# First expert's tokens as the one-hot product writes them: turned, in 24 products into two banks

## The chip, the cores and the metric

One core of one Trainium2 chip. The time is the device time of one execution, in microseconds (us); the median of three runs counts. TensorE, VectorE, ScalarE, GpSimd and SyncE run their own instruction streams and wait for each other on semaphores.

## What is computed

One step of a two-layer decoder trunk, for 256 prompt tokens and 8 sample tokens (264 in all, of width 1024). Each layer is a mixer (layer 0: gated DeltaNet and mLSTM heads, layer 1: S5), a LayerNorm, a mixture of 16 experts, and a LayerNorm. The change is in the mixture of experts:

```python
def moe(x, router_w, router_b, w_gate, w_up, w_down):
    logits = jnp.einsum('bld,de->ble', x.astype(F32), router_w.astype(F32))
    probs = jax.nn.softmax(logits, axis=-1)
    ...                       # best group, top-2 experts in it, weights comb
    hid = jax.nn.silu(jnp.einsum('bld,edf->blef', x, w_gate)) * jnp.einsum('bld,edf->blef', x, w_up)
    hid = hid * comb[..., None].astype(hid.dtype)
    return jnp.einsum('blef,efd->bld', hid, w_down)
```

## The kernel before

Everything is fp32; the program issues one product, and the profile shows two matmul passes for it (one for a transpose). The 264 tokens lie in three tiles, 128, 128 and 8 rows. Each expert works on up to SLOT = 64 tokens at a time: their rows are gathered, turned into features by 128-column chunks (DC = 8 chunks), multiplied by gate and up weights (L1934 and L1935, 8 chunks each, on the two halves of the array), gated (silu on ScalarE, L1989, product on VectorE, L2018), turned again (L1881), multiplied by the down weights (L1958, L1959), evicted to `ypair`, and spread back to the tokens by a product (L1976, L1980) for each pair of experts.

For experts 1 to 15 the rows come by an indirect DMA of GpSimd (L2042) from `x_dram`, a copy of the rows in DRAM that SyncE's queue stores in three transfers (L1816, called x_rows); `xg` holds them, and PE turns them in `pe_tokens` (L1881) into bank 4, from where ScalarE copies them to `xgT` (L1985).

Expert 0 doesn't wait for the gather. While routing is worked out (`route_pe`, `route_dve`), VectorE makes `first_slot` (L1761), a one-hot matrix of tokens by slots, for the first expert. `pe_first_rows` (L1895) multiplies it with `xperm`, the permuted rows: 3 tiles by 2 halves, 6 products, with the one-hot matrix as the weights (64 columns) and 512 columns of `xperm` moved. The result, the 64 gathered rows, lies in bank 7, columns 0 to 511 on partitions 0 to 63 and the rest on partitions 64 to 127. ScalarE copies one half (L1903) and VectorE the other (L1909) to `first_rows`, which lies in `ypair[0]`. `xperm` lies over the same memory, so both copies first wait until x_rows has been read out (`x_rows` 48). Then `pe_first_tokens` turns the rows by eight transposes (L1881), and `act_tokens` copies bank 4 to `xgT[0]` (L1985). Gate/up of expert 0 waits for that.

The order on PE is written out by hand: `route_pe` issues the mask products (L1632 to L1636), fillers (`keep_busy`, L311: products of 512 columns whose result nobody reads), `pe_first_rows`, the list product (L1642, 6 products, from which VectorE makes the indices of all gathers, L1789 and L1791), and then `moe_pe` issues the first tokens, gate/up of expert 0, `route_sel_pe` (L1650), the tokens of expert 1, and so on. VectorE does `dve_first_rows` between `lists` (L1765) and the weights and indices. ScalarE does `act_first_rows` and `act_tokens` ahead of its loop over experts.

The weights of an expert (two halves of gate and up, 1 MB each of four, and 2 MB of down) are loaded by SyncE's queue into three slots in layer 1 and fewer in layer 0; a load from expert 3 on is issued when PE has released the slot (`gu_half`, `gu_done`, `down_done`).

Of the kernel before, what the change touches and what calls it, by code (L numbers as in the profile page):

```python
# [89 lines left out]
def build(nc, io, out, book):  # L90

    ctx = ExitStack()
    with ctx:
# [3 lines left out]
        def sem(name):  # L97
            if name not in sems:
                sems[name] = ctx.enter_context(nc.semaphore(name))
            return sems[name]  # L100
# [26 lines left out]
        def tok(t):  # L127

            return P if t < TT else NS
# [1487 lines left out]
        def route_pe(t, tag):  # L1617
            t.wait_ge(sem("router_in"), 32)
            for i in range(TT):
                t.wait_ge(*ac.at(f"{tag}xT_in{i}"))  # L1620
                for k in range(DC):
                    nc.tensor.matmul(ps[:, 1, i * NE:(i + 1) * NE], xT[:, k, i * P:(i + 1) * P], router[:, k], start=k == 0, stop=k == DC - 1)
            xT_rest_pe(t, tag)
            t.wait_ge(*dv.at(f"{tag}xT_rest"))
            for k in range(DC):
                last = nc.tensor.matmul(ps[0:NS, 1, TT * NE:3 * NE], xT[:, k, SEQ:], router[:, k], start=k == 0, stop=k == DC - 1)
            last.then_inc(*pe.done(f"{tag}logits"))
            keep_busy(0, 6)
            t.wait_ge(*dv.at(f"{tag}mask"))
            flat_mask = rt(9, 48)  # L1630

            nc.tensor.matmul(ps[:, 1, 0:48], before, flat_mask, start=True, stop=False)  # L1632
            t.wait_ge(*dv.at(f"{tag}tiles_so_far"))
            nc.tensor.matmul(ps[:, 1, 0:48], ones, rt(4, 48), start=False, stop=True).then_inc(*pe.done(f"{tag}pos"))
            t.wait_ge(*dv.at(f"{tag}all_tiles"))
            nc.tensor.matmul(ps[:, 6, 256:256 + NE], ones, rt(5, 48)[:, 0:NE], start=True, stop=True).then_inc(*pe.done(f"{tag}total"))  # L1636

            keep_busy(0, 2)
            pe_first_rows(t, tag)
            t.wait_ge(*dv.at(f"{tag}lists"))  # L1640
            for n in range(6):
                last = nc.tensor.matmul(ps[0:SLOT, 1, 128:128 + LISTS], at_slot[:, n], list_value[:, n], start=n == 0, stop=n == 5)  # L1642
            last.then_inc(*pe.done(f"{tag}lists"))
# [14 lines left out]
        def route_dve(v, tag):  # L1658
# [104 lines left out]
            v.wait_ge(*dv.last())  # L1763
            per_list = lambda a: a.rearrange("p i j -> p (i j)").unsqueeze(2).to_broadcast([P, 6, LISTS])
            nc.vector.tensor_tensor(list_value, in_list, per_list(value_f), ALU.mult).then_inc(*dv.done(f"{tag}lists"))  # L1765
            dve_first_rows(v, tag, 0 if tag == "n0" else 1)
            weight, both = rt(6, 3, 2), rt(0, 48)[:, 0:3]
            for j in range(2):
                nc.vector.tensor_tensor(rt(10 + j), hot[j], e, ALU.mult).then_inc(*dv.done())  # L1769
# [112 lines left out]
                          **(dict(start=True, stop=True) if c == 0 else {}))  # L1882
            last.then_inc(signal, 1)

        first_rows = ypair[0][0:SLOT]

        def pe_first_rows(t, tag):

            for i in range(3):
                t.wait_ge(*po.at(f"{tag}rows{i}"))  # L1890
            t.wait_ge(*dv.at(f"{tag}first_slot"))
            for i in range(3):
                n = tok(i)
                for half in range(2):
                    last = nc.tensor.matmul(ps[SLOT * half:SLOT * half + SLOT, 7, :], first_slot[0:n, i, 0], xperm[0:n, i, 512 * half:512 * half + 512],  # L1895
                                            start=i == 0, stop=i == 2)
            last.then_inc(*pe.done(f"{tag}first_rows"))

        def act_first_rows(a, tag, l):

            a.wait_ge(sem(f"x_rows{l}"), 48)
            a.wait_ge(*pe.at(f"{tag}first_rows"))
            nc.scalar.copy(first_rows[:, 0:512], ps[0:SLOT, 7, :]).then_inc(*ac.done(f"{tag}first_rows"))  # L1903

        def dve_first_rows(v, tag, l):

            v.wait_ge(sem(f"x_rows{l}"), 48)
            v.wait_ge(*pe.at(f"{tag}first_rows"))
            nc.vector.tensor_copy(first_rows[:, 512:D], ps[SLOT:P, 7, :]).then_inc(*dv.done(f"{tag}first_rows"))  # L1909

        def pe_first_tokens(t, tag, l):

            t.wait_ge(*ac.at(f"{tag}first_rows"))
            t.wait_ge(*dv.at(f"{tag}first_rows"))
            to_features(ps[:, 4], first_rows, DC, sem(f"tokens_done{l}"))

        def pe_tokens(t, l, k, u, s):

# [6 lines left out]
        def pe_gate_up(t, l, k, u, s):  # L1925
            w = waits(t, l)
            w("xgT_done", k + 1)
            if later(k):
                w("hid_done", k)
            slot, nth = gu_slot(l, k, u, s)  # L1930
            for c in range(DC):
                if c % 4 == 0:
                    t.wait_ge(sem(f"w_gu{c // 4}{slot}_{l}"), nth * 32)
                nc.tensor.matmul(ps[0:SLOT, 5, :], xgT[s][:, c], gate_w[slot][:, c], start=c == 0, stop=c == DC - 1)  # L1934
                last = nc.tensor.matmul(ps[SLOT:P, 5, :], xgT[s][:, c], up_w[slot][:, c], start=c == 0, stop=c == DC - 1)  # L1935
                if c == 3:
                    last.then_inc(sem(f"gu_half{l}"), 1)
            last.then_inc(sem(f"gu_done{l}"), 1)
# [44 lines left out]
        def act_tokens(a, l, k, u, s):  # L1983
            waits(a, l)("tokens_done", k + 1)
            nc.scalar.copy(xgT[s].rearrange("p a b -> p (a b)"), ps[:, 4, :]).then_inc(sem(f"xgT_done{l}"), 1)  # L1985
# [69 lines left out]
        def at_expert(k):  # L2055

            return k, k // 2, k % 2
# [38 lines left out]

        def moe_pe(t, tag, l):

            pe_first_tokens(t, tag, l)
            for k in range(NE):  # L2100
                pe_gate_up(t, l, *at_expert(k))
                if k == 0:
                    route_sel_pe(t, tag)
                if k % 2 == 1 and k >= 3:
                    pe_combine(t, l, k // 2 - 1, k - 2, slice(0, P), (k // 2 - 1) % 2)
                if k + 1 < NE:
                    pe_tokens(t, l, *at_expert(k + 1))
                if k > 0:
                    pe_down(t, l, *at_expert(k - 1))
                pe_units(t, l, *at_expert(k))  # L2110
                if k == 0:
                    t.wait_ge(*dv.at(f"{tag}sel"))
                    residual_pe(t, 0, 0)
            pe_down(t, l, *at_expert(NE - 1))

            def more(k, e, u, s):
                for part in (pe_tokens, pe_gate_up, pe_units, pe_down):
                    part(t, l, k, u, s)
                pe_combine(t, l, None, k, slice(SLOT * s, SLOT * s + SLOT), 0)
            further_rounds(t, tag, more)  # L2120
            pe_combine(t, l, PAIRS - 1, NE - 1, slice(0, P), (PAIRS - 1) % 2)

        def moe_act(a, tag, l):

            act_first_rows(a, tag, l)
            act_tokens(a, l, *at_expert(0))
            a.wait_ge(*dv.at(f"{tag}list_sel"))
            for k in range(NE):
                act_silu(a, l, *at_expert(k))
                if l == 0 and k == NE // 2:  # L2130
                    ln_load(a, "ln_ffn_g", "ln_ffn_b", 0, "n0")
                if k + 1 < NE:
                    act_tokens(a, l, *at_expert(k + 1))
                if k > 0:
                    act_y(a, l, *at_expert(k - 1))
            act_y(a, l, *at_expert(NE - 1))

            def more(k, e, u, s):
                for part in (act_tokens, act_silu, act_y):
                    part(a, l, k, u, s)  # L2140
            further_rounds(a, tag, more)

        def moe_dve(v, tag, l):

            for k in range(NE):
                dve_hid(v, l, *at_expert(k))
                if k == 0:
                    route_sel(v, tag)
                if k > 0:
                    dve_y(v, l, *at_expert(k - 1))  # L2150
                dve_hidT(v, l, *at_expert(k))
                dve_spread(v, l, k, k % 2, (sel[:, 0, k:k + 1], sel[:, 1, k:k + 1]))
                if l == 0 and k == 2:
                    s5_turn_start(v)
                if l == 0 and 3 <= k < 15:
                    s5_turn_step(v, (k - 3) // 2, (k - 3) % 2)
            dve_y(v, l, *at_expert(NE - 1))

            def more(k, e, u, s):
                for part in (dve_hid, dve_hidT, dve_y):  # L2160
                    part(v, l, k, u, s)
                dve_spread(v, l, k, s, (selc[:, 0:1], selc[:, 1:2]))
            further_rounds(v, tag, more)
            waits(v, l)("combined", NE)
            with if_crowded(v, tag):
                waits(v, l)("combined", NE * ROUNDS)
# [677 lines left out]
```

## Time and profile before

| | |
|---|---|
| median of 3 runs | 963.6 us (963.37 to 964.43) |
| profiled execution | 964.52 us |
| its span | 962.7 us |
| PE busy | 890.9 us (93%) |
| PE weight loads busy | 478.0 us (50%) |
| VectorE busy | 395.9 us (41%) |
| ScalarE busy | 172.7 us (18%) |
| GpSimd busy | 216.9 us (23%) |
| mean granted clock of TensorE | 0.956 of full speed |
| moved by DMA | 277.32 MB, mean 288 GB/s |

Busy PE is not PE at its peak, since matmuls are pipelined and thin ones wait for their weight loads. The page's rows of 40 slices cover 24 us each; a digit is the busy share in tenths. The chain of work that ended last says where time is on the path, and the granted clock by stretch says at which of its two levels (1.2 or 2.4 GHz) TensorE ran there. Layer 0's experts run from about 300 to 557 us, layer 1's from about 708 us to the end.

### The profile page before, as it was taken

The numbers are of one execution on the slowest core, as the hardware profiler recorded it, in microseconds if no ns is written. First come the engines' busy times: TensorE is split into PE (matmuls) and PEld (weight loads), VectorE is DVE, ScalarE is ACT, GpSimd is POOL, SyncE is SP. The second block draws the span as 40 slices with busy tenths as digits, with TensorE's granted clock in tenths as the row PEclk, the third lists the DMA queues.
The fourth block names the chain that finished last, engine by engine and source line by source line (L and its number), as shares of the span: only waits on it lengthen the run. The fifth ranks groups of instructions, "written<-read, shape, count | busy, mean of one in ns | idle before, by whom it ended". The sixth has DMA issues, their size and how long they took to land.

```text
span 962.7 us, 13215 instructions
## 1 busy us (share of the span) xinstructions
PE 890.9 (93%) x5404; PEld 478.0 (50%) x5404; DVE 395.9 (41%) x812; ACT 172.7 (18%) x310; POOL 216.9 (23%) x322
## 2 busy tenths in 40 slices
PE   8899998998997999899989769999799999999992
PEld 5788887984463433333333258644543333333330
DVE  4489845735645212122233267844252212121125
ACT  0402234223020111111101143012101111111011
POOL 4469997301120510101000020001102100110000
PEclk9999999997988999999999988999799999999997
DMA  9527655903969879999999947466939999999952
GB/s 272 113 93 261 224 175 151 294 13 114 316 231 380 343 291 353 405 412 404 401 405 425 413 173 209 142 237 243 364 137 355 417 400 402 399 409 406 408 243 90
DMA packets 100830, 277.32 MB, mean 288 GB/s; under 512 B 25368, under 2 KB 61670, under 8 KB 80150
## 3 DMA queue, kind: packets, MB, share of 16 engines
q1 hardware_dynamic: 89882, 256.26, 70.6%
q10 hardware_dynamic: 8484, 16.09, 4.9%
q0 software_dynamic: 2400, 4.07, 1.4%
q8 instruction: 46, 0.75, 0.3%
q14 instruction: 18, 0.15, 0.0%
HBM read 260.97 MB, written 18.01 MB: 290 GB/s over the span
## 4 chain that ended last, share of the span: by engine, by line
PE 78%; DMA 9%; DVE 8%; ACT 2%; issue 2%; SPq 0%; POOL 0%; DVEq 0%; ACTq 0%
PE ps L1934 21%; PE ps L361 11%; PE ps L1958 10%; DMA ring<-in_moe_w_up 6%; PE ps L2629 5%; PE ps L1976 5%; PE ps L1881 4%; PE ps L864 3%; DMA x_rows<-work 2%; PE ps L2493 2%; PE ps L2509 1%; PE ps L1571 1%; PE ps L1980 1%; DVE work L1534 1%; DVE work L1518 1%
## 5 line engine op out<-in xcount | busy, mean ns | idle before, releaser
L1934 PE MATMUL ps<-ring,work 128*64 128x512 f32 x416 | 187.3, 602 | 5.4 <-DMA ring<-in_moe_w_up 4.0
L1935 PE MATMUL ps<-ring,work 128*64 128x512 f32 x416 | 187.3, 603 | 0.0
L361 PE MATMUL ps<-work,ring 128*128 128x264 f32 x512 | 118.7, 392 | 3.0 <-ACT work L468 3.0
L2018 DVE TENSOR_TENSOR work<-ps,work 64x512 f32<-64x512 f32 x32 | 33.7, 1054 | 207.2 <-ACT work L1989 207.2
L1934 PEld LDWEIGHTS ps<-ring,work 128*64 128x64 f32 x416 | 55.2, 138 | 115.4 <-issue 106.1
L361 PEld LDWEIGHTS ps<-work,ring 128*128 128x128 f32 x512 | 97.3, 192 | 21.4 <-ACT work L468 3.4
L1958 PE MATMUL ps<-ring,work 128*64 128x512 f32 x216 | 100.1, 607 | 7.0 <-issue 5.6
L1959 PE MATMUL ps<-ring,work 128*64 128x512 f32 x216 | 100.2, 607 | 0.0
L1334 POOL TENSOR_TENSOR ring<-ring 128x512 f32<-128x512 f32 (+5 forms) x76 | 93.2, 1242 | 10.8 <-DVE ring L1330 7.5
L2028 DVE COPY work<-ps 64x512 f32<-64x512 f32 x32 | 22.2, 694 | 157.3 <-PE ps L1959 157.3
L2039 POOL COPY work<-work 64x1 int32<-64x1 int32 x30 | 6.1, 202 | 324.2 <-PE ps L1881 277.9
L1976 PE MATMUL ps<-work 128*128 128x512 f32 x128 | 59.3, 605 | 4.5 <-issue 3.7
L1881 PEld LDWEIGHTS ps<-const,work 64*128 64x128 f32 x448 | 39.1, 161 | 48.1 <-issue 43.0
L1989 ACT ACTIVATE work<-ps 64x512 f32<-64x512 f32 x32 | 18.8, 589 | 220.2 <-PE ps L1935 220.2
L2629 PE MATMUL ps<-ring,work 128*128 128x512 f32 x128 | 57.4, 597 | 0.6 <-DMA ring<-in_s_w_glu_b 0.6
L1958 PEld LDWEIGHTS ps<-ring,work 128*64 128x64 f32 x216 | 27.7, 138 | 56.4 <-issue 53.3
L1935 PEld LDWEIGHTS ps<-ring,work 128*64 128x64 f32 x416 | 55.2, 138 | 0.0
L1881 PE MATMUL ps<-const,work 64*128 64x64 f32 x448 | 47.8, 244 | 4.6 <-DVE work L1769 3.1
L1976 PEld LDWEIGHTS ps<-work 128*128 128x128 f32 x128 | 23.0, 189 | 40.0 <-issue 40.0
L1934 PE MATMUL ps<-work 128*64 128x512 f32 x96 | 42.6, 595 | 0.0
L1935 PE MATMUL ps<-work 128*64 128x512 f32 x96 | 42.6, 595 | 0.0
L532 DVE SCALAR_TENSOR_TENSOR work<-work 128x256 f32<-128x256 f32 x36 | 40.3, 1120 | 1.3
(488 smaller groups left out, 1213.2 us busy)
## 6 DMA issues: line engine op xcount, KB each, us to landing
ring<-in_moe_w_down SPq DMA_DIRECT2D x27, 2048.0 KB, 19.1
ring<-in_moe_w_gate SPq DMA_DIRECT2D x52, 1024.0 KB, 12.4
ring<-in_moe_w_up SPq DMA_DIRECT2D x52, 1024.0 KB, 14.6
ring<-in_w_in ACTq DMA_DIRECT2D x6, 2048.0 KB, 8.6
work<-in_moe_w_gate SPq DMA_DIRECT2D x12, 1024.0 KB, 16.9
work<-in_moe_w_up SPq DMA_DIRECT2D x12, 1024.0 KB, 19.1
work<-in_moe_w_down SPq DMA_DIRECT2D x5, 2048.0 KB, 22.5
s_out_mats<-ring SPq DMA_DIRECT2D x8, 640.0 KB, 5.1
```

What stands on the lines that cost most here:

```text
L361: last = nc.tensor.matmul(ps[:, proj_bank(j), 0:T], win[g % 2][:, k, (j % 4) * P:(j % 4 + 1) * P], xT[:, k], start=k == 0, stop=k == DC - 1)
L532: nc.vector.scalar_tensor_tensor(y, raw[:, c, w:w + SEQ], convT[:, c, 24 + w:25 + w], y, ALU.mult, ALU.add).then_inc(*dv.done())
L864: last = nc.tensor.matmul(ps[:, 2 * i + n, :], rows_of(oT[:, k], i), wout[:, k, n * 512:(n + 1) * 512], start=False, stop=k == 7)
L1334: tt = lambda o, a, b, op, name=None: nc.gpsimd.tensor_tensor(o, a, b, op).then_inc(*po.done(name))
L1881: last = op(bank[:, c * SLOT:(c + 1) * SLOT], rows[0:SLOT, c * P:(c + 1) * P], ident[0:SLOT, 0:SLOT], **(dict(start=True, stop=True) if c ...
L1934: nc.tensor.matmul(ps[0:SLOT, 5, :], xgT[s][:, c], gate_w[slot][:, c], start=c == 0, stop=c == DC - 1)
L1935: last = nc.tensor.matmul(ps[SLOT:P, 5, :], xgT[s][:, c], up_w[slot][:, c], start=c == 0, stop=c == DC - 1)
L1958: nc.tensor.matmul(ps[0:SLOT, 7, :], hidT[s][:, c], down_w[l][slot][:, c, 0:512], start=c == 0, stop=c == 3)
L1959: last = nc.tensor.matmul(ps[SLOT:P, 7, :], hidT[s][:, c], down_w[l][slot][:, c, 512:D], start=c == 0, stop=c == 3)
L1976: last = nc.tensor.matmul(ps[:, 2 * i + n, :], S[rows, i * P:(i + 1) * P], y[rows, 512 * n:512 * n + 512], **flags)
L2018: nc.vector.tensor_tensor(hid[s][0:SLOT].rearrange("t (c p) -> t p c", c=4), strided(ps[SLOT:P, 5, :]), strided(sg[s][SLOT:P]), ALU.mult). ...
L2629: last = nc.tensor.matmul(ps[:, GLU_BANK[h, i][ab], :], gyT[:, k, i * P:(i + 1) * P], glu_w(h, k)[:, ab], start=k == 0, stop=k == DC - 1)
```

## The change

`pe_first_tokens` now makes the turned tokens directly: for each chunk c of 128 features and each tile i, `xperm`'s 128 columns are the weights and the 64 columns of the one-hot matrix are moved. That is 24 products. Chunks 0 to 3 go to bank 4 and raise `tokens_done`; chunks 4 to 7 go to bank 7 and raise `first_tokens`. ScalarE copies the first bank to `xgT[0][:, 0:4]`, VectorE the second to `xgT[0][:, 4:8]`; gate/up of expert 0 waits for the second before its chunk 4. The gathered rows, their two copies, the eight transposes and the copy behind them are gone. The waits for x_rows move: on ScalarE ahead of `act_silu` of expert 1, on VectorE behind `route_sel`, ahead of the first write to `hidT`. The call stands where `pe_first_rows` stood, ahead of the list product; `moe_pe` no longer begins with the transposes.

```diff
-            pe_first_rows(t, tag)
+            pe_first_tokens(t, tag, int(tag == "n2"))
...
-            dve_first_rows(v, tag, 0 if tag == "n0" else 1)
+            dve_first_tokens(v, tag)
...
-        def pe_first_rows(t, tag):
+        def pe_first_tokens(t, tag, l):
 
             for i in range(3):
                 t.wait_ge(*po.at(f"{tag}rows{i}"))
             t.wait_ge(*dv.at(f"{tag}first_slot"))
-            for i in range(3):
-                n = tok(i)
-                for half in range(2):
-                    last = nc.tensor.matmul(ps[SLOT * half:SLOT * half + SLOT, 7, :], first_slot[0:n, i, 0], xperm[0:n, i, 512 * half:512 * half + 512],
-                                            start=i == 0, stop=i == 2)
-            last.then_inc(*pe.done(f"{tag}first_rows"))
-
-        def act_first_rows(a, tag, l):
-
-            a.wait_ge(sem(f"x_rows{l}"), 48)
-            a.wait_ge(*pe.at(f"{tag}first_rows"))
-            nc.scalar.copy(first_rows[:, 0:512], ps[0:SLOT, 7, :]).then_inc(*ac.done(f"{tag}first_rows"))
...
-        def pe_first_tokens(t, tag, l):
-
-            t.wait_ge(*ac.at(f"{tag}first_rows"))
-            t.wait_ge(*dv.at(f"{tag}first_rows"))
-            to_features(ps[:, 4], first_rows, DC, sem(f"tokens_done{l}"))
+            for c in range(DC):
+                for i in range(3):
+                    n = tok(i)
+                    last = nc.tensor.matmul(ps[:, 4 + 3 * (c // 4), (c % 4) * SLOT:(c % 4 + 1) * SLOT], xperm[0:n, i, c * P:(c + 1) * P],
+                                            first_slot[0:n, i, 0], start=i == 0, stop=i == 2)
+                if c == 3:
+                    last.then_inc(sem(f"tokens_done{l}"), 1)
+            last.then_inc(*pe.done(f"{tag}first_tokens"))
+
+        def act_first_tokens(a, l):
+
+            waits(a, l)("tokens_done", 1)
+            nc.scalar.copy(xgT[0][:, 0:4].rearrange("p a b -> p (a b)"), ps[:, 4, 0:4 * SLOT]).then_inc(sem(f"xgT_done{l}"), 1)
+
+        def dve_first_tokens(v, tag):
+
+            v.wait_ge(*pe.at(f"{tag}first_tokens"))
+            nc.vector.tensor_copy(xgT[0][:, 4:8].rearrange("p a b -> p (a b)"), ps[:, 7, 0:4 * SLOT]).then_inc(*dv.done(f"{tag}first_tokens"))
...
+                if isinstance(k, int) and k == 0 and c == 4:
+                    t.wait_ge(*dv.at(f"n{2 * l}first_tokens"))
...
-            pe_first_tokens(t, tag, l)
...
-            act_first_rows(a, tag, l)
-            act_tokens(a, l, *at_expert(0))
+            act_first_tokens(a, l)
             a.wait_ge(*dv.at(f"{tag}list_sel"))
             for k in range(NE):
+                if k == 1:
+                    a.wait_ge(sem(f"x_rows{l}"), 48)
                 act_silu(a, l, *at_expert(k))
...
                     route_sel(v, tag)
+                    v.wait_ge(sem(f"x_rows{l}"), 48)
```

## Rows read from the trace of the kernel before

**Rows 1.** The page: granted clock in 40 slices of 24 us.

```profile
PEclk9999999997988999999999988999799999999997
```

**Rows 2.** Chain that ended last, layer 0: start us, us, what.

```profile
284.13 19.75 DMA x_rows<-work
...
306.56 1.11 PE ps L1934
307.68 0.85 PE ps L1934
```

**Rows 3.** Timeline, layer 0: start us, us, engine, line, op, tiles, count [idle before].

```profile
297.73 2.94 PE L1895 MATMUL ps<-work 128*64 128x512 f32 x12 [1.43 <-DVE work L1761]
...
300.60 1.04 PE L1642 MATMUL ps<-work 128*64 128x80 f32 x12
...
303.90 0.69 DVE L1909 COPY work<-ps 64x512 f32<-64x512 f32 x1 [5.06 <-DMA x_rows<-work]
...
307.89 1.20 POOL L2042 DMA_INDIRECT work<-x_rows,work  x1 [0.23 <-issue]
...
316.10 1.81 PE L1650 MATMUL ps<-work 128*64 128x160 f32 x24
...
317.83 0.87 PE L1881 MATMUL ps<-const,work 64*128 64x64 f32 x9
```

**Rows 4.** Line 2042, the gather issued at 307.9: issue to landing.

```profile
DMA to landing us min/median/max: 6.6/6.6/6.6
```

**Rows 5.** Timeline, layer 1.

```profile
708.66 2.94 PE L1895 MATMUL ps<-work 128*64 128x512 f32 x12 [1.27 <-DVE work L1761]
...
711.53 1.04 PE L1642 MATMUL ps<-work 128*64 128x80 f32 x12
...
714.07 0.64 PE L1934 MATMUL ps<-ring,work 128*64 128x512 f32 x1 [0.68 <-ACT work L1985]
```

**Rows 6.** Single lines: duration ns min/median/max, first and last start, forms.

```profile
L735 PE MATMUL ps<-const,ring x16: 175/256/256, 205.3 to 206.9; 128*128 128x8 f32 x16
...
L383 PE MATMUL ps<-work,const x8: 277/278/278, 64.3 to 65.1; 4*128 4x40 f32 x8
...
L2023 DVE COPY work<-ps x32: 424/425/425, 320.2 to 937.4; 128x256 f32<-128x256 f32 x32
```

**Rows 7.** By stretch: us, PE, PEld, DVE, ACT, POOL busy, PEclk, DMA share, GB/s.

```profile
279.00:281.00 2.00, 2.00 (x19) 2.00 (x19) 1.83 (x4) 1.72 (x5) 0.00 (x0) 1.00 0.98 410
281.00:283.00 2.00, 2.00 (x12) 2.00 (x11) 1.04 (x2) 1.27 (x1) 0.95 (x1) 0.54 1.04 438
...
301.70:304.70 3.00, 0.00 (x0) 0.00 (x0) 0.80 (x3) 0.58 (x1) 0.00 (x0) 1.00 1.02 427
306.60:309.00 2.40, 2.40 (x6) 0.72 (x8) 0.98 (x2) 0.00 (x0) 2.08 (x3) 0.50 1.03 434
...
217.00:219.00 2.00, 2.00 (x16) 1.40 (x8) 0.29 (x1) 0.53 (x1) 1.23 (x2) 1.00 0.00 0
...
219.70:223.00 3.30, 3.30 (x18) 3.30 (x17) 0.80 (x2) 0.58 (x1) 0.11 (x1) 0.50 0.00 0
...
697.00:700.50 3.50, 3.50 (x7) 1.50 (x5) 2.65 (x16) 0.24 (x1) 0.00 (x0) 0.50 0.73 205
701.00:704.00 3.00, 3.00 (x8) 1.14 (x6) 2.55 (x14) 0.00 (x0) 0.00 (x0) 1.00 0.92 393
```

**Rows 8.** The same view over longer stretches of the two expert stages.

```profile
312.00:316.00 4.00, 4.00 (x20) 1.26 (x18) 0.00 (x0) 0.00 (x0) 0.00 (x0) 1.00 0.55 168
...
324.00:328.00 4.00, 4.00 (x22) 1.31 (x20) 0.00 (x0) 0.00 (x0) 3.77 (x9) 1.00 0.55 143
...
340.00:352.00 12.00, 12.00 (x66) 4.53 (x64) 2.75 (x5) 1.75 (x3) 3.38 (x5) 1.00 0.48 169
...
372.00:553.00 181.00, 166.92 (x813) 62.19 (x811) 48.33 (x82) 22.08 (x38) 12.18 (x28) 0.99 1.01 409
760.00:920.00 160.00, 160.00 (x807) 60.19 (x801) 28.52 (x44) 19.86 (x34) 13.16 (x30) 1.00 1.01 407
```

More of the change, by code:

```diff
@@ L1883, in to_features @@
             last.then_inc(signal, 1)
-        first_rows = ypair[0][0:SLOT]
-        def pe_first_rows(t, tag):
+        def pe_first_tokens(t, tag, l):
             for i in range(3):
@@ L1891, in pe_first_rows @@
             t.wait_ge(*dv.at(f"{tag}first_slot"))
-            for i in range(3):
-                n = tok(i)
-                for half in range(2):
-                    last = nc.tensor.matmul(ps[SLOT * half:SLOT * half + SLOT, 7, :], first_slot[0:n, i, 0], xperm[0:n, i, 512 * half:512 * half + 512],
-                                            start=i == 0, stop=i == 2)
-            last.then_inc(*pe.done(f"{tag}first_rows"))
-        def act_first_rows(a, tag, l):
-            a.wait_ge(sem(f"x_rows{l}"), 48)
-            a.wait_ge(*pe.at(f"{tag}first_rows"))
-            nc.scalar.copy(first_rows[:, 0:512], ps[0:SLOT, 7, :]).then_inc(*ac.done(f"{tag}first_rows"))
[L1905 to L1909, printed above, removed]
-        def pe_first_tokens(t, tag, l):
-            t.wait_ge(*ac.at(f"{tag}first_rows"))
-            t.wait_ge(*dv.at(f"{tag}first_rows"))
-            to_features(ps[:, 4], first_rows, DC, sem(f"tokens_done{l}"))
+            for c in range(DC):
[12 more added lines that the diff above has]
+            nc.vector.tensor_copy(xgT[0][:, 4:8].rearrange("p a b -> p (a b)"), ps[:, 7, 0:4 * SLOT]).then_inc(*dv.done(f"{tag}first_tokens"))
         def pe_tokens(t, l, k, u, s):
```

## Prediction

> **What bounds the kernel now.** I read the page first: its clock row [rows 1] says that TensorE runs at full clock except in a few short stretches; the view by stretch, that the DMA engines are full in the larger part of both expert stages [rows 8]. Then the chain of work that ended last, around the two places that the diff touches. The reader is to see there that the two layers differ although the code is the same. In layer 0 the chain hangs for 19.75 us on one transfer, the store of the rows to DRAM (x_rows), then on the eviction at 303.90 [rows 3], the eight transposes and a copy, until the first gate/up product at 306.56 [rows 2]. In layer 1 the store has landed long before, and the chain runs through the engines: one-hot product at 708.66, list product at 711.53, gate/up at 714.07 [rows 5]. The timelines of the two places give the starts [rows 3, 5], the views of single lines the cost of a pass [rows 6], and the busy time by stretch the granted clock and the DMA share [rows 7, 8]. From 760 to 920 TensorE is busy 160.00 of 160 us [rows 8]: what layer 1 gains or loses at its start reaches the end one for one.
>
> **Removed.** Per layer: 12 passes of the gathering product (two passes per fp32 product, 2.94 us of PE in both layers [rows 3, 5]), two copies of 512 columns, eight transposes and the copy behind them, and in front of the copies the wait for x_rows. The copies waited for x_rows only because their target lies on the rows being stored; the new target does not.
>
> **Added.** Per layer: 24 products, so 48 passes, each with 128 columns of weights and only 64 columns moved. Such a pass is set by the weight load. The nearest rows: 16 passes with 128 rows and 8 columns start between 205.3 and 206.9, 15 steps in 1.6 us, 0.107 us each. For the third tile, with 8 rows, the nearest row has 4 rows and 40 columns: 8 passes start between 64.3 and 65.1, again 0.11 us [rows 6]. So few rows save nothing, and I take 48 x 0.107 = 5.14 us. If the 16 short passes cost as little as a list pass (64 weight columns, 12 in 1.04 us, 0.087 [rows 3]) it would be 0.3 us less. Then two copies of 256 columns on ScalarE and VectorE (0.42 us for such a one [rows 6]). The first runs under the second half of the products, the second under the list product, which lasts 0.97 us from start to start of what follows; both cost nothing as long as the list product stays behind them. Without it the second would cost some 0.5 us.
>
> The Trainium skill (TensorE: Matmul & The Clock Gate, on the per-matmul spacing in a stream) gives about 81 ns for a stream of load and matmul pairs of 128 columns. By it the 48 passes would be an estimated 3.9 us, 1.2 us less in each layer. The rows of this trace show 107 ns, and I keep to them.
>
> **Layer 1, at full clock.** Both versions start on the same signal, at 708.66. 708.66 + 5.14 + 0.97 = 714.77 against 714.07 [rows 5]: 0.70 us later. The two evictions and the transposes that go were mostly under the list product already, and 48 thin passes take more than 12 wide ones and nine short ones.
>
> **Layer 0, at full clock.** 297.73 + 5.14 + 0.97 = 303.84 for the first gate/up against 306.56 [rows 2, 3]. Before it TensorE stood idle for 3 us (0.00 of 3.00 busy from 301.7), and the clock was at half behind that, 0.50 from 306.6 [rows 7]: seven pairs of passes went through at up to 0.85 us instead of 0.43, and gate/up ended at 316.26 (the chain hands over 0.16 us into the next line's 316.10 [rows 3]), 9.70 us after it began. At full clock it takes 16 x 0.43 = 6.88 us and ends at 310.72: 5.54 us earlier. What is late next is the gather of expert 1's tokens. VectorE makes its indices behind the new copy, which starts at 297.73 + 5.14 + 0.15 = 303.02 instead of 303.90 and is 0.27 us shorter. So the gather goes out 1.15 us earlier than 307.89, at 306.74, and lands 6.6 us later [rows 4], at 313.3. Its transposes would be ready to run at 310.72 + 1.57 = 312.3 (they began 1.57 us after gate/up's end, 317.83 [rows 3]). So 1.0 us of stall is given back: gain 4.5 us. The store of the rows, landed at 303.88, still stands ahead of the gather and of VectorE and ScalarE a little later, and is done by then.
>
> Does the gain survive the DMA? From 372 to 553 the engines are full (share 1.01) and TensorE waits for weights. But earlier there is room which only TensorE's late releases cause: 1.8 us in 312 to 316, 1.8 in 324 to 328, 6.2 in 340 to 352 [rows 8], 9.8 in all. Earlier releases close 4.5 us of it, so the full part starts and ends 4.5 us earlier. I take the gain as kept.
>
> Sum at full clock: -4.5 + 0.7 = -3.8 us.
>
> **The clock.** This is the term that decides. In layer 0 the products of line 1622 (128 columns of weights, 16 moved) began at 278.9. TensorE was busy 2.00 of 2.00 us from 279 and 2.00 of 2.00 from 281, and yet the granted clock went from 1.00 to 0.54 (a fall at about 281.1, 2.2 us after they began). It also fell behind a run of products with 4 rows: 2.00 of 2.00 busy from 217, clock 0.50 from 219.7 [rows 7]. So the full clock (2.4 GHz) was lost twice under back-to-back work: once under passes that a 128-column weight load sets, once under passes with few rows. The new stream has both: all its passes wait for such loads, a third of them have 8 rows, and TensorE has stood idle for 1.43 and 1.27 us just before it [rows 3, 5]. The work that it replaces was 512 columns wide, and kept the clock. I expect the level of 1.2 GHz to come in during the 48 passes in both layers. I place it after two thirds, between the row's 2.2 us and the end of the stream; the rest of the stream and the list product then cost double. For how long gate/up stays slow the rows give 4.0 us (wide products from 697.0, clock 1.00 from 701) to 5.3 us (306.56 to 311.9) [rows 7]; I take 4.0.
> Layer 1: 0.70 + 16 x 0.107 (1.71) + 0.97 + 4.0 us of gate/up at half clock (2.0) = 5.4 us later.
> Layer 0: 297.73 + 32 x 0.107 + 16 x 0.213 = 304.56; + 1.94 = 306.5; 4.0 us for 4.7 pairs, 11.3 pairs x 0.43 = 4.86; end 315.4 against 316.26: 0.9 us gained, and the gather is in time.
> Sum: 5.4 - 0.9 = +4.5 us. Its bounds: a fall after 2.2 us (21 passes at full clock) with 5.3 us slow in gate/up costs layer 1 0.70 + 27 x 0.107 + 0.97 + 2.65 = 7.2 and makes layer 0 end at 317.2, 0.9 late: +8.1. A fall as the list product begins, with 2 us slow in gate/up, costs layer 1 0.70 + 0.97 + 1.0 = 2.7 and lets layer 0 end at 312.7, 3.5 early: -0.8.
>
> **Rivals.**
> 1. The clock holds in both layers: -3.8 us, 959.8. For it: the moved columns (64) are four times those of line 1622, and layer 0's idle 3 us goes, the very thing after which the clock fell. It ends on the other side, and the point from which it decides is whether the clock row shows 1.00 from 297 to 320 and from 708 to 722.
>    The Trainium skill (TensorE: Matmul & The Clock Gate, section on HAM oscillation) names idle gaps as what lets the clock drop; by that rule, with no gap left, this rival is what happens. The rows above, a fall at full busy time, disagree.
> 2. Only layer 1 falls, where the idle time ahead and the thin stream come together: 5.4 - 4.5 = +0.9, 964.5. Only layer 0 falls: 0.7 - 0.9 = -0.2, 963.4.
> 3. The clock holds but the DMA absorbs layer 0's gain, because the loads that are due earlier meet the ones queued: +0.7, 964.3. Against it stand the 9.8 us of idle DMA.
> 4. The change doesn't free layer 0, because the gather's own wait takes the place of the one removed (a landing 9 us after issue instead of 6.6): 2.4 us more stall than above, -1.4, 962.2.
>
> **How the numbers follow.** The profiled execution took 964.52 us with a span of 962.7; the median shown is 963.6. The sum is made on the trace's own times, 964.5 + 4.5 = 969.0, and moved by 0.9 to the median: 968.1. Chances: clock falls in both layers 0.52 (its own range 962.8 to 971.7), holds in both 0.20, layer 1 alone 0.12, layer 0 alone 0.05, absorbed 0.06, gather 0.05. Anything within 0.2% (1.9 us) can't be told from no change. Faster: the case that holds, a little of the others, 0.21. Slower: the first case but its lower end, some of layer 1 alone, 0.52. Same: 0.27. Range 959.5 to 971.0: it reaches down through the middle of the case that holds, and leaves out the last of the first case's upper end.
>
> **What would show it.** In the profile after: 48 passes of the new line in about 5.1 us if at full clock and over 7 if not; the first gate/up at 303.8 or 306.5 in layer 0 and 5 to 8 us behind the stream's start in layer 1; no wait for x_rows ahead of it; the clock row at 281 to 312 and 708 to 722; the DMA idle share between 304 and 352 smaller by the gain. A pass well under 0.107 us, or a clock that stays at 1.00 through the stream, makes the prediction wrong, and the second turns its sign.

## The result and the profile after

| | before | after |
|---|---|---|
| median | 964.0 us (963.4 to 964.7, 4 runs) | 973.0 us (971.4 to 976.9, 4 runs) |
| profiled execution, span | 964.5, 962.7 us | 976.9, 974.7 us |
| mean granted clock in it | 0.956 | 0.943 |

The change makes the kernel 1.0% slower: ratio 1.010, interval 1.0071 to 1.0129. The forecast had the sign and the rough cause (968.1, slower), but the size was too small by half and the time lies above the range. A ratio compares only executions within 1.5% of their kernel's fastest; that leaves out two of the four of run e3 and none elsewhere.

The page of the kernel after, against [rows 1]. The 13th slice (from 292 us, layer 0's stream) stands at 7 where it was 8, and the 30th (from 707 us, layer 1's stream) at 7 where it was 9. The 17th (from 390 us, among layer 0's experts) stands at 8 where it was 9:

```profile
PEclk9999999997977999899999979999679999999997
```

The timeline of TensorE after, at the two places of [rows 3, 5]. The new products are L1893, the list product is still L1642, gate and up are now L1928 and L1929:

```profile
297.60 10.73 PE L1893 MATMUL ps<-work 128*128 128x64 f32 x48 [1.28 <-DVE work L1761]
308.26 1.73 PE L1642 MATMUL ps<-work 128*64 128x80 f32 x11
309.65 1.11 PE L1929 MATMUL ps<-ring,work 128*64 128x512 f32 x1
...
317.36 1.92 PE L1650 MATMUL ps<-work 128*64 128x160 f32 x24
...
711.61 11.44 PE L1893 MATMUL ps<-work 128*128 128x64 f32 x48 [1.27 <-DVE work L1761]
722.98 1.73 PE L1642 MATMUL ps<-work 128*64 128x80 f32 x11
724.38 1.11 PE L1929 MATMUL ps<-ring,work 128*64 128x512 f32 x1
...
732.93 1.91 PE L1650 MATMUL ps<-work 128*64 128x160 f32 x24
```

The 48 passes take 10.7 and 11.4 us. The chain shows them whole: the store of the rows, 19.75 us in [rows 2], has gone from it, and the new products stand there instead.

```profile
297.09 0.37 DVE work L1761
297.60 10.73 PE ps L1893 x48
308.33 1.66 PE ps L1642 x11
```

The busy time by stretch (us, PE, PEld, DVE, ACT, POOL, granted clock, DMA share, GB/s) says at which level they ran:

```profile
297.60:300.60 3.00, 3.00 (x20) 2.60 (x20) 1.08 (x2) 0.00 (x0) 0.00 (x0) 1.00 0.97 389
301.60:308.20 6.60, 6.60 (x25) 5.70 (x24) 0.00 (x0) 0.37 (x1) 0.00 (x0) 0.50 1.02 428
...
711.60:713.80 2.20, 2.19 (x15) 1.93 (x15) 1.09 (x2) 0.00 (x0) 0.00 (x0) 1.00 0.00 0
714.20:722.80 8.60, 8.60 (x32) 7.42 (x32) 0.00 (x0) 0.37 (x1) 0.00 (x0) 0.50 0.01 2
723.00:727.50 4.50, 4.50 (x21) 3.18 (x22) 3.20 (x13) 0.00 (x0) 1.68 (x3) 0.50 0.00 0
```

Two things are to be seen. At full clock 15 passes take 2.20 us, 0.15 us each and not 0.107. And in both layers the clock falls to half inside the stream, 2.4 us (layer 1) and some 3.5 us (layer 0) after its start, with TensorE busy all the time. From the start of the stream to the end of gate/up it is now 317.36 - 297.60 = 19.8 us in layer 0, where it was 316.10 - 297.73 = 18.4 [rows 3], and 732.93 - 711.61 = 21.3 us in layer 1, where the same steps of before took 12.3 (708.66 [rows 5] to the end of gate/up at 720.99). That is +1.4 and +9.0, 10.4 us in all. The median moved by 9.0; the execution shown is the slowest of the four, and its span is 12.0 us longer than the one before (974.7 against 962.7). The rest, 1.7 us, lies between the two places: from the end of gate/up in layer 0 to the start of layer 1's stream it is 711.61 - 317.36 = 394.3 us where it was 708.66 - 316.10 = 392.6. Two stretches at half clock stand there, where the kernel before has one, from 404.1 to 407.4:

```profile
403.50:410.20 6.70, 5.07 (x12) 1.65 (x14) 0.00 (x0) 0.00 (x0) 0.25 (x1) 0.50 1.01 393
506.00:509.20 3.20, 3.20 (x10) 0.86 (x8) 0.00 (x0) 0.00 (x0) 0.00 (x0) 0.50 0.98 410
```

They need not be the change's: run e7 below, which has no new stream, shows such a pair too (396.5 to 403.4 and 498.9 to 502.3).

### The profile page after: what moved, and what is told of

It is laid out like the page before. It is cut to its first block, busy times and chain, and to the rows that moved or that the text cites. A ratio compares the mean times of both kernels' runs of the same rounds, so it can differ in the third digit from the quotient of the medians.

```text
span 974.7 us, 13319 instructions
## 1 busy us (share of the span) xinstructions
PE 909.2 (93%) x5458; PEld 499.9 (51%) x5458; DVE 395.2 (41%) x812; ACT 171.1 (18%) x308; POOL 216.9 (22%) x322
## 4 chain that ended last, share of the span: by engine, by line
PE 83%; DVE 8%; DMA 3%; ACT 3%; issue 2%; SPq 0%; POOL 0%; DVEq 0%; ACTq 0%
PE ps L1928 21%; PE ps L1952 11%; PE ps L361 11%; PE ps L2624 6%; PE ps L1970 6%; PE ps L1881 4%; PE ps L864 3%; DMA ring<-in_moe_w_up 3%; PE ps L1893 2%; PE ps L1929 2%; PE ps L2488 2%; PE ps L2504 1%; PE ps L1571 1%; PE ps L1622 1%; PE ps L1974 1%
## 5 line engine op out<-in xcount | busy, mean ns | idle before, releaser
L1928 PE MATMUL ps<-ring,work 128*64 128x512 f32 x416 | 188.1, 605 | 2.8 <-DMA ring<-in_moe_w_up 2.8
L1929 PE MATMUL ps<-ring,work 128*64 128x512 f32 x416 | 188.4, 606 | 0.0
L1928 PEld LDWEIGHTS ps<-ring,work 128*64 128x64 f32 x416 | 55.8, 139 | 102.9 <-issue 97.7
L361 PEld LDWEIGHTS ps<-work,ring 128*128 128x128 f32 x512 | 97.4, 192 | 21.3 <-ACT work L468 3.4
L1929 PEld LDWEIGHTS ps<-ring,work 128*64 128x64 f32 x416 | 55.7, 139 | 6.5 <-issue 6.5
L1881 PE MATMUL ps<-const,work 64*128 64x64 f32 x430 | 45.8, 244 | 1.5 <-ACT work L1979 0.8
L1928 PE MATMUL ps<-work 128*64 128x512 f32 x96 | 42.6, 595 | 0.0
L1929 PE MATMUL ps<-work 128*64 128x512 f32 x96 | 42.6, 595 | 0.0
```

Of the source, the lines that this page charges most:

```text
L361: last = nc.tensor.matmul(ps[:, proj_bank(j), 0:T], win[g % 2][:, k, (j % 4) * P:(j % 4 + 1) * P], xT[:, k], start=k == 0, stop=k == DC - 1)
L1881: last = op(bank[:, c * SLOT:(c + 1) * SLOT], rows[0:SLOT, c * P:(c + 1) * P], ident[0:SLOT, 0:SLOT], **(dict(start=True, stop=True) if c ...
```

## The experiments

The first question is why a pass costs 0.15 us at full clock. The kernel before already showed it, in a view that I had not read for this: its weight loads (PEld) in layer 0.

```profile
298.61 0.17 PEld L1895 LDWEIGHTS ps<-work 128*64 128x64 f32 x2 [0.26 <-issue]
299.60 0.19 PEld L1895 LDWEIGHTS ps<-work 8*64 8x64 f32 x4 [0.81 <-issue]
```

From the load at 298.61 to the first load with 8 rows two passes of 512 columns run, 2 x 0.43 = 0.86 us, but it comes 0.99 us later: 0.13 us goes where the weights change from 128 rows to 8. The old product makes that change once and goes back once, the new stream goes 128, 128, 8 rows for every chunk: 16 changes counting the way back each time. Theory A: a change of rows costs about 0.15 us on top of the passes.

### e1_tile_major: the same products, four changes of rows

```diff
-            for c in range(DC):
-                for i in range(3):
-                    n = tok(i)
...
+            for h in range(2):
+                bank = ps[:, 4 + 3 * h, 0:4 * SLOT]
+                nc.tensor.matmul(bank.rearrange("p (a b) -> p a b", a=16), ident, rt(4)[:, 0].unsqueeze(1).to_broadcast([P, 16, NE]), start=True, stop=False)
+                for i in range(3):
+                    n = tok(i)
+                    for c in range(4 * h, 4 * h + 4):
+                        last = nc.tensor.matmul(ps[:, 4 + 3 * h, (c % 4) * SLOT:(c % 4 + 1) * SLOT], xperm[0:n, i, c * P:(c + 1) * P],
+                                                first_slot[0:n, i, 0], start=False, stop=i == 2 and c % 4 == 3)
...
```

(Four changes where the change has 16, if the last way back, to the list product, is counted in both.)

> The changed kernel with its 24 products in another order: in each bank the 128-row tiles first and the 8-row tile last, so that the number of rows of the weights changes 3 times in the stream instead of 16. So that the chunks of a bank can be summed side by side, each bank first gets a product with a moved operand of zeros (256 columns, some 0.43 us each, 0.86 us in all). Theory A (each change of rows costs about 0.15 us beside the passes themselves, at full clock, and the half clock adds the rest): the 48 passes lose 13 x 0.15 = 2.0 us at full clock and up to 4 us at half clock per layer; the gate/up products of expert 0 begin 1 to 3 us earlier after the stream's start than in the changed kernel, and the time is about 968 to 971. Theory B (a pass with 128 weight columns of this tile is slow by itself, whatever the order): the stream is as long as before, plus 0.9 us, and the time is about 974.

Measured: 968.8 us, ratio 1.0056 (1.0034 to 1.0077), where the change itself has 1.010. The timeline of layer 0, the gather of expert 1 from issue to landing as the chain has it, and the stretch view of both layers:

```profile
298.57 2.92 PE L1896 MATMUL ps<-work 128*128 128x64 f32 x24
301.42 0.70 PE L1892 MATMUL ps<-work,const 128*128 128x256 f32 x2
301.96 2.92 PE L1896 MATMUL ps<-work 128*128 128x64 f32 x24
...
308.65 7.91 DMA work<-x_rows,work
...
316.60 0.87 PE L1881 MATMUL ps<-const,work 64*128 64x64 f32 x9 [2.23 <-DMA work<-x_rows,work]
...
298.10:304.80 6.70, 6.70 (x52) 6.34 (x52) 1.04 (x2) 0.37 (x1) 0.00 (x0) 1.00 1.01 404
709.60:716.30 6.70, 6.70 (x52) 6.35 (x52) 1.05 (x2) 0.37 (x1) 0.00 (x0) 1.00 0.01 2
```

24 passes, 8 of them with 8 rows, take 2.85 us from start to start: 24 x 0.107 = 2.57 and 0.28 for two changes of rows, 0.14 each. So the passes with 8 rows are not slow in themselves, the changes are; theory B falls. The clock stayed at full in both streams of this execution, which I had not counted on (the mean granted clock of the ten timed ones lay between 0.948 and 0.962, so it need not be so in each). In layer 0 gate/up is over by 312.5, 14.4 us after the stream's start where it was 18.4 before, but the transposes of expert 1 then wait 2.23 us for the gather, the step that the prediction had named as late next; it took 7.9 us to land, not 6.6 [rows 4]. Gate/up of expert 1 begins 322.31 - 298.06 = 24.3 us after the stream's start, as before (321.92 - 297.73 = 24.2): with the clock held through the stream and gate/up, nothing of layer 0's gain is left there. The lower time left two readings: the order did it, or the two wide products of zeros did.

### e8_zero_old_order: the zeros, but the old order

```diff
             for c in range(DC):
+                if c % 4 == 0:
+                    nc.tensor.matmul(ps[:, 4 + 3 * (c // 4), 0:4 * SLOT].rearrange("p (a b) -> p a b", a=16), ident,
+                                     rt(4)[:, 0].unsqueeze(1).to_broadcast([P, 16, NE]), start=True, stop=True)
                 for i in range(3):
```

> The changed kernel with the two products of zeros of the tile-major run (256 columns, about 0.5 us each) ahead of each bank, but the 24 products in their own order, chunk by chunk, with 16 changes of rows. It separates the order from the added wide work. Theory A (the order did it: the changes of rows cost 0.15 us each and drag the clock down): the stream takes 8.6 us or more at full clock and 11 to 12.5 us where the clock falls, it falls in at least one layer, and the time is about 1.5 to 2 us above the changed kernel. Theory D (the wide products held the clock in the tile-major run): the clock stays at full in both layers, gate/up begins 9.6 us after the stream's start and runs at full speed, and the time is about 966 to 968.

Measured: 977.3 us, ratio 1.0133 (1.0116 to 1.015). By stretch:

```profile
299.00:301.00 2.00, 2.00 (x7) 1.58 (x7) 0.00 (x0) 0.37 (x1) 0.00 (x0) 0.50 1.12 422
...
710.30:711.70 1.40, 1.40 (x12) 1.20 (x10) 0.54 (x1) 0.00 (x0) 0.00 (x0) 1.00 0.00 0
711.90:715.50 3.60, 3.60 (x14) 3.04 (x13) 0.00 (x0) 0.00 (x0) 0.00 (x0) 0.50 0.00 0
```

The clock falls in both layers, in layer 1 some 2 us after the stream's start. Theory D falls. With the same products (but for their start and stop flags) and the same zeros, the order is worth 977.3 - 968.8 = 8.5 us (each measured beside its own executions of before; by the ratios 0.8%). Against the change itself the zeros cost about 3 us by the ratios, where theory A had 1.5 to 2; the intervals overlap.

### e2_full_rows: no changes of rows at all

```diff
-                    n = tok(i)
+                    j, n = min(i, 1), P
-                    last = nc.tensor.matmul(ps[:, 4 + 3 * (c // 4), (c % 4) * SLOT:(c % 4 + 1) * SLOT], xperm[0:n, i, c * P:(c + 1) * P],
-                                            first_slot[0:n, i, 0], start=i == 0, stop=i == 2)
+                    last = nc.tensor.matmul(ps[:, 4 + 3 * (c // 4), (c % 4) * SLOT:(c % 4 + 1) * SLOT], xperm[0:n, j, c * P:(c + 1) * P],
+                                            first_slot[0:n, j, 0], start=i == 0, stop=i == 2)
```

> The changed kernel with the third tile's products (8 rows) replaced by the second tile's once more, so that all 48 passes have 128 rows and none changes the rows; the first expert's tokens then lack the sample rows and count the second tile twice, which leaves the work otherwise the same. Theory A (changes of rows cost 0.15 us each; the clock falls because a third of the passes have few rows): the stream takes 5.1 to 5.3 us at full clock in both layers, gate/up begins 6.2 us after the stream's start, and the time is about 960 to 962. Theory C (64 moved columns behind a 128-column load are enough to lose the clock): the changes go, but the clock still falls in the stream; the stream takes 7 to 8 us, gate/up starts slow, and the time is about 966 to 969.

Measured: 968.9 us, ratio 1.0041 (1.0026 to 1.0055). The stream in layer 0, then the stretches of layer 1:

```profile
294.71 5.54 PE L1893 MATMUL ps<-work 128*128 128x64 f32 x48 [1.27 <-DVE work L1761]
...
706.60:708.60 2.00, 2.00 (x19) 2.00 (x19) 1.01 (x2) 0.00 (x0) 0.00 (x0) 1.00 0.00 0
709.00:714.80 5.80, 5.80 (x29) 5.80 (x28) 0.00 (x0) 0.37 (x1) 0.00 (x0) 0.50 0.02 3
```

48 passes in 5.54 us (0.115 each, 0.112 from one start to the next) at full clock: the price of a pass was nearly right, and the changes were what was missing. The time is what theory C had, but neither theory has the clock right: it held through the stream in layer 0 and fell in layer 1, 2.2 us after the start, with passes of 128 rows only. So changes and short rows are not needed for the fall; a stream of 64 moved columns behind 128-column loads can lose the clock, and does so in one place and not in another. What tells the two places apart stays open. In layer 0, where the clock held, the gather again took back what gate/up had won: it landed 7.9 us after its issue, the transposes waited 2.89 us, and gate/up of expert 1 began 319.35 - 294.71 = 24.6 us after the stream's start.

### e3_fillers: wide products between the thin ones

```diff
+                if c % 2 == 1:
+                    keep_busy(0, 1)
```

> The changed kernel with a wide product that nobody reads (512 columns, two passes, about 0.86 us) behind every second chunk of the 24 products, four per layer. Theory A (the half clock is the larger part of the loss): the clock stays at full in both layers; the stream takes 7.6 + 3.4 = 11 us, gate/up begins about 12 us after the stream's start, as in the changed kernel, but runs at full speed: 6.9 us. Layer 1's gate/up ends about 2.7 us earlier than in the changed kernel, layer 0's about 1 us; time about 969 to 970. Rival (the clock falls anyway, as the fillers are too few): the stream takes 14 us or more and the time is 978 or more.

Measured: four executions, 973.4, 979.1, 990.2 and 990.3 us; the ratio of the two lower ones is 1.0117 (1.0076 to 1.0157). The profile is of the one with 990.3, and its reading holds for that one alone:

```profile
296.12 2.58 PE L1893 MATMUL ps<-work 128*128 128x64 f32 x12 [1.27 <-DVE work L1761]
298.62 2.08 PE L311 MATMUL ps<-const 128*128 128x512 f32 x2
300.49 3.23 PE L1893 MATMUL ps<-work 128*128 128x64 f32 x12
...
300.60:303.60 3.00, 3.00 (x13) 2.58 (x11) 0.00 (x0) 0.00 (x0) 0.00 (x0) 0.50 1.06 433
```

The rival was right for this execution: the clock was at half from the first microsecond or so and stayed there, and the fillers cost double as well. The mean granted clock was 0.959 in the fastest execution and 0.939 in one of the slowest, so the clock did not fall in the same way every time. As a remedy it is worthless: even the fastest is no faster than the median of the change (973.0).

What a change of rows costs at half clock is read best from the changed kernel, in four whole chunks of layer 1:

```profile
714.68:721.32 6.64, 6.64 (x25) 5.70 (x24) 0.50 0.00 0
```

These are 24 passes with eight changes, by the 24 weight loads. Without changes a pass takes 0.213 us at this clock (e2, layer 1), 24 of them 5.11 us; 1.53 us are left, 0.19 for each change.

### e4_layer0_only: which layer loses

```diff
-            pe_first_tokens(t, tag, int(tag == "n2"))
+            if tag == "n0":
+                pe_first_tokens(t, tag, 0)
+            else:
+                pe_first_rows(t, tag)
```

and the same choice on ScalarE and VectorE.

> The changed kernel's way in layer 0 alone; layer 1 is as in the kernel before. Theory (the loss is layer 1's: there the change replaces a path without a stall, in layer 0 the stall that it removes pays for most of the longer stream): layer 0's gate/up ends 1 to 2 us later after its stream's start than before (about 19.9 us against 18.5), and the time is within 2 us of the kernel before, while the changed kernel is 9 us slower. Rival (both layers lose alike, as the DMA part doesn't pass on what the removed stall gives): the time is 4 to 5 us above the kernel before.

Measured: 966.4 us, ratio 1.0025 (1.0008 to 1.0043), so 2.4 us (0.8 to 4.1) for layer 0. The rest of the change's 9 us, some 6.6, is layer 1's, if the two simply add up. In layer 0:

```profile
296.09 10.48 PE L1899 MATMUL ps<-work 128*128 128x64 f32 x48 [1.43 <-DVE work L1764]
...
315.91 1.91 PE L1653 MATMUL ps<-work 128*64 128x160 f32 x24
```

19.8 us from the stream's start to gate/up's end, as in the change (19.8) and 1.4 us more than before. The theory holds in the trace, and the time can't be told from its bound of 2 us: the removed stall pays for most of the longer stream in layer 0, and nothing pays in layer 1.

### e5_before_filler: the price of the idle time's half clock

```diff
+            if l == 0:
+                keep_busy(0, 3)
             pe_first_tokens(t, tag, l)
```

> The kernel before with three wide products that nobody reads (512 columns, 0.86 us each, 2.6 us in all) in layer 0, between the list product and the transposes, where TensorE otherwise stands idle for 3 us waiting for the store of the rows. It prices the half clock behind that idle time alone. Theory (the idle time is what brings the half clock there, and an earlier end of gate/up reaches the end of the kernel): gate/up still begins at about 306.6 but runs at full clock, ends 2.7 us earlier, and the time is about 2 to 2.7 us below the kernel before. Rival (the DMA absorbs it, or the gather of expert 1, landing at 314.5, takes it back): less than 1.5 us.

Measured: ratio 0.9995 (0.9981 to 1.0008), no difference that can be told. The stretches:

```profile
302.10:303.90 1.80, 0.00 (x0) 0.00 (x0) 0.78 (x3) 0.58 (x1) 0.00 (x0) 1.00 1.00 346
305.60:309.00 3.40, 3.40 (x10) 0.97 (x12) 1.20 (x2) 0.00 (x0) 2.34 (x3) 0.56 1.02 429
309.60:313.00 3.40, 3.40 (x18) 1.16 (x16) 0.00 (x0) 0.00 (x0) 0.00 (x0) 1.00 0.69 183
```

The fillers ran as soon as TensorE was free, so 1.8 us of idle time was left behind them, and the clock still fell for a while. Gate/up took 8.6 us (9.5 before, 6.9 at full clock). The run doesn't decide the question that it was made for: of 0.9 us gained in gate/up nothing shows in the time, whose interval reaches from 1.8 us less to 0.8 us more.

### e6_rows_in_xg: the kernel before without its stall

```diff
-        first_rows = ypair[0][0:SLOT]
+        first_rows = xg[1][0:SLOT]
...
         def dve_first_rows(v, tag, l):
 
-            v.wait_ge(sem(f"x_rows{l}"), 48)
...
-            nc.gpsimd.memset(xg[1], 0.0).then_inc(*po.done(f"{tag}xg_zero1"))
...
+            waits(pool, l)("tokens_done", 1)
```

ScalarE's wait for x_rows goes in the same way, and both stand now where the changed kernel has them.

> The kernel before, with the gathered rows of expert 0 put into the second gather buffer (xg[1]) instead of over the rows that are being stored, so that the two copies don't wait for the store to DRAM. The waits for the store move to where the changed kernel has them; the gather for expert 1 waits until the transposes of expert 0 are done, and the buffer isn't zeroed any more. Theory (layer 0's 3 us of idle time and the half clock behind it are the whole prize, and the DMA passes it on): layer 0's gate/up begins at about 303.3 instead of 306.6 and runs at full clock, ends 5 to 6 us earlier; layer 1 is unchanged; time about 958 to 959. Rival (the DMA engines, full from 372 on, absorb it): the gate/up of expert 0 is earlier by as much, but the time stays within 1 us of the kernel before.

Measured: 963.6 us, ratio 0.9984 (0.9970 to 0.9998).

```profile
303.21 0.64 PE L1932 MATMUL ps<-ring,work 128*64 128x512 f32 x1 [0.68 <-ACT work L1983]
...
310.12 1.81 PE L1650 MATMUL ps<-work 128*64 128x160 f32 x24
313.18 0.87 PE L1881 MATMUL ps<-const,work 64*128 64x64 f32 x9 [1.24 <-DMA work<-x_rows,work]
314.82 0.88 PE L1881 MATMUL ps<-const,work 64*128 64x64 f32 x5 [0.77 <-ACT work L1983]
315.63 3.31 PE L1571 MATMUL ps<-work,const 128*128 128x512 f32 x4
```

Gate/up begins at 303.21 as worked out (303.3) and ends 6.0 us before it did. Then the gather of expert 1, the step which the prediction had named as late next, takes 1.24 us of it, and the clock falls behind that wait: the four passes of L1571 take 3.31 us, not the 1.98 of the runs at full clock. Expert 1's first gate/up, at 318.87, is only 3.05 us earlier than it was (321.92). The time is 1.5 us (0.2 to 2.9) under the kernel before, neither the 5 of the theory nor clearly the less than 1 of the rival. Where the 3 us go from there the trace tells, in layer 1, which the expectation had taken as unchanged:

```profile
705.65 2.94 PE L1895 MATMUL ps<-work 128*64 128x512 f32 x12 [1.27 <-DVE work L1761]
...
725.37 0.64 PE L1932 MATMUL ps<-ring,work 128*64 128x512 f32 x1
...
711.00:714.00 3.00, 2.96 (x8) 1.00 (x10) 1.32 (x4) 0.00 (x0) 2.12 (x3) 0.50 0.00 0
```

Layer 1's stream still begins 3.0 us earlier (708.66 before). But gate/up of expert 0 begins at half clock there, where it ran at full clock before, and expert 1 begins only 1.4 us earlier (726.81 before). The span is 1.3 us shorter. Why the clock fell in that place is not shown.

### e7_lists_first: the gather earlier

On top of the last: `route_lists` right behind `dve_first_rows`, and in layer 0 one `keep_busy(2, 1)` ahead of expert 1's tokens.

> The kernel before with the rows of expert 0 in the second gather buffer, as in the run with the rows in xg, and two edits for the stall that showed there (1.24 us of waiting for expert 1's gather, with the clock at half behind it): VectorE makes the indices of the gathers right behind its copy, ahead of the weights, and in layer 0 one wide product that nobody reads stands ahead of the tokens of expert 1. Theory (the gather comes behind the indices): the gather goes out about 1 us earlier, the stall is 0.3 us or less, the clock stays at full through expert 0 and 1 of layer 0, and the time is 1 to 3 us below that of the run with the rows in xg, about 961. Rival (the gather waits for its place behind the weights in the DMA queues, and lands at about 313 whatever its issue): the stall only turns into the filler, and the time is that of the run with the rows in xg.

Measured: 963.1 us, ratio 0.9981 (0.9967 to 0.9995).

```profile
303.52 0.30 POOL L2037 COPY work<-work 64x1 int32<-64x1 int32 x1 [19.75 <-DMA x_rows<-work]
304.75 1.20 POOL L2040 DMA_INDIRECT work<-x_rows,work  x1 [0.23 <-issue]
...
309.71 1.81 PE L1650 MATMUL ps<-work 128*64 128x160 f32 x24
311.45 1.13 PE L311 MATMUL ps<-const 128*128 128x512 f32 x2
312.51 0.87 PE L1881 MATMUL ps<-const,work 64*128 64x64 f32 x9
...
316.58 0.64 PE L1932 MATMUL ps<-ring,work 128*64 128x512 f32 x1
```

The gather went out at 304.75 (305.49 in the run before this one) and could go no earlier: it now waits for the store of the rows itself. No wait is left behind the filler, and the clock stayed at full through both experts. Against the last run the gain is below what can be told (0.9981 against 0.9984, the intervals overlap almost wholly), so theory and rival aren't parted by time. These two are the fastest kernels here, both 0.2% under the kernel before (the intervals end just below no change) and 1% under the change.

## Why the prediction was wrong, point by point

- **What bounds the two places.** Right. The stall for the store goes in layer 0, layer 1 had none to give, and what layer 1 loses reaches the end.
- **The price of the stream.** The step that failed: "I take 48 x 0.107 = 5.14 us", with "few rows save nothing" for the tile of 8 rows. The price of a pass was nearly right (0.112 us from start to start in the run with full rows), and that of a short pass too. But I priced the passes by rows in which like stands next to like. The new stream changes the rows of its weights 16 times, at 0.14 us each at full clock and 0.19 at half: 2.2 us per layer if the clock holds, which makes the stream 7.6 us long, and 2.8 us as it ran. The trace of before had such a change there and back, in weight loads that I had not read.
- **The clock.** The mechanism, named as the term that decides, was right: it fell inside the stream in both layers. Its place was mis-sized. I put it after 32 passes; it came after about 16 in layer 1 and 23 in layer 0: in time (2.4 us) inside the bound that I gave (2.2 us), in passes of layer 1 not (21). The two terms may not be independent: with 4 changes instead of 16 the clock held in both layers of the profiled execution, with the old order and the same zeros it fell in both, and the mean granted clocks agree (0.948 to 0.962 in ten executions, 0.947 to 0.949 in four). But without any change it fell in layer 1 all the same (e2). What makes it fall stays open. Gate/up was slow for less time than I took: 8.5 us long in layer 1 and 7.7 in layer 0, against 8.9.
- **The sum.** Layer 1: +5.4 expected, +9.0 seen. Layer 0: -0.9 expected, +1.4 seen. The two streams were 8.3 us longer than I took (11.37 and 10.66 us against 6.85 and 6.83). Of that the changes of rows are 5.5, the earlier fall, 25 passes more at half clock, 2.7, and the pass of 0.112 the rest. A shorter list product (1.40 us each against 1.94) and slow stretch behind it took back 2.6.
- **The rivals.** The case in which the clock holds did not come, and it would not have gained either. The changes of rows and the dearer pass alone add 2.5 us per layer and turn its -3.8 into +1.1 (worked out, not run). And the 4.5 us that it counts for layer 0 aren't there: in e1 and e2 the clock held through layer 0's stream and gate/up, and expert 1's gate/up still began 24.3 and 24.6 us after the stream's start, 24.2 before. I let the gather land 6.6 us after its issue and cost 1.0 us of waiting; it took 7.9 us in both, with the DMA engines full meanwhile (share 1.01 and 1.00, where it was 0.64 before), and the waits were 2.2 and 2.9 us, with the clock at half behind them. That is the rival of the gather's own wait, to which I had given 0.05. So the sign of the change never hung on the clock alone, as I had written; layer 1 alone would lose 0.7 + 2.5 = 3.2 us with the clock held (worked out). In e1, where it held in both layers of the profiled execution, the span was 3.1 us longer than before.
- **DMA absorbs the gain.** Not tested by the change, which has no gain. The two kernels without the stall bring expert 1's gate/up in layer 0 forward by 3.05 and 5.3 us (318.87 and 316.58 against 321.92), and in the same traces layer 1's stream by 3.0 and 4.3 us (705.65 and 704.38 against 708.66). So the full DMA engines between them pass on the whole of it in e6 and most of it in e7, as I had taken it. The time moved by 1.5 and 1.4 us (0.16 and 0.19%). In e6 the other half is lost in layer 1, at half clock behind the stream; for e7 the trace doesn't say, as it is of an execution (960.2 us) 2.9 us under its median.

## What to carry to other kernels

A thin product is priced by its neighbours too: count how often a stream changes the number of rows of its weights, and keep tiles of one size together. Before wide products are traded for many narrow ones to save an eviction and some transposes, ask what they do to the clock, and look for a cheaper way to the same end: here another buffer for the rows removed the same stall, with the wide products kept. And when a stall goes, price what is late next at the load that it will then meet: here the gather took 7.9 us to land where the DMA share was 1.00, 6.6 where it was 0.64, and 5.0 in the changed kernel, where it was 0.51.

## What the runs showed that was not expected

- A change between weights of 128 rows and of 8 rows costs 0.13 to 0.14 us of TensorE's time at full clock (0.13 in the kernel before, 0.14 in e1) and 0.19 us at half clock (the changed kernel, layer 1), on top of passes of 0.11 and 0.21 us.
- The clock fell to 1.2 GHz with TensorE busy 100% of the time, 2.2 us into a stream of 128-row passes with 64 moved columns in one layer (e2), and held through the same stream in the other.
- With the clock held through layer 0's gate/up (e1, e2), the first expert was done earlier and the second wasn't: the gather, issued while the DMA engines were full, took 7.9 us to land instead of 6.6.
- The time of one kernel can spread widely: four executions of e3 lay between 973.4 and 990.3 us.
